# Gate and up projections of an FFN in seven half-size products instead of eight, in a tuned three-mixer layer kernel

## The reference

```python
x = x + g1 * _rmsnorm(mix, p['g_post_mix'])            # x1 below
h = _rmsnorm(x, p['g_pre_ffn']) * (1.0 + sc2) + sh2
f = (jax.nn.silu(h @ p['w_ffn_gate']) * (h @ p['w_ffn_up'])) @ p['w_ffn_down']
x = x + g2 * _rmsnorm(f, p['g_post_ffn'])
```

## Time and profile before

| | before |
|---|---|
| runs shown | 1843.31, 1847.68, 1849.92 us |
| median | 1847.68 us |
| the profiled execution's own time | 1849.39 us |
| its span | 1847.5 us (1.9 us lie around it) |
| mean granted TensorE clock | 0.98 of full speed |
| matmuls on PE | 12300 |

### The profile page before, as it was taken

One profiled execution on the slowest core, in us unless ns is written; L12 is line 12 of the kernel. 1 busy time (PEld: TensorE's weight loads), 2 busy tenths in 40 slices (PEclk: granted clock), 3 DMA queues, 4 the chain that ended last, 5 costly groups with the idle time before them and its releaser, 6 DMA issues.

```text
span 1847.5 us, 30614 instructions
## 1 busy us (share of the span) xinstructions
PE 1758.9 (95%) x12300; PEld 1645.6 (89%) x12300; DVE 879.7 (48%) x1584; ACT 587.1 (32%) x1209; POOL 108.4 (6%) x170
## 2 busy tenths in 40 slices
PE   5899899999999999999999899999899999999996
PEld 2678898898999999999997799999899999999995
DVE  2654425555465655333443344555564344434445
ACT  4333323333433332233333343232342222222222
POOL 0000101110122220000000000000000000000001
PEclk8899899999999999999999999999999999999998
DMA  9463232257623435754355745445223322322211
GB/s 344 152 245 124 79 116 94 79 174 216 217 89 130 140 128 177 249 164 141 119 163 185 251 168 179 157 147 168 92 69 103 92 69 69 87 74 69 90 49 57
DMA packets 237308, 254.65 MB, mean 138 GB/s; under 512 B 14983, under 2 KB 220487, under 8 KB 234096
## 3 DMA queue, kind: packets, MB, share of 16 engines
q1 hardware_dynamic: 208944, 223.85, 37.9%
q10 hardware_dynamic: 28224, 28.85, 4.6%
HBM read 194.11 MB, written 58.55 MB: 137 GB/s over the span
## 4 chain that ended last, share of the span: by engine, by line
PE 77%; issue 9%; DVE 5%; DMA 4%; DVEq 2%; ACT 1%; SPq 1%; POOLq 1%; POOL 0%; ACTq 0%; PEldq 0%; PEld 0%
PE pj_acc L374 14%; PE pj_acc L376 14%; PE pj_acc L375 14%; PE pj_acc L381 5%; PE pj_acc L382 5%; PE pj_acc L383 5%; PE mx L2796 3%; PE mx L2798 3%; PE mx L2797 3%; DMA ar_w<-in_w_ada 2%; PE mx L1753 2%; PE mx L2235 1%; PE mx L2244 1%; PE mx L1250 1%; PE mx L1263 1%
## 5 line engine op out<-in xcount | busy, mean ns | idle before, releaser
L374 PE MATMUL pj_acc<-pj_act_hi,pj_lo 128*128 128x320 f32 x1808 | 580.4, 321 | 5.1 <-DVE pj_act_lo L685 4.1
L375 PE MATMUL pj_acc<-pj_act_lo,pj_hi 128*128 128x320 f32 x1808 | 562.4, 311 | 0.0
L376 PE MATMUL pj_acc<-pj_act_hi,pj_hi 128*128 128x320 f32 x1808 | 562.3, 311 | 0.0
L374 PEld LDWEIGHTS pj_acc<-pj_act_hi,pj_lo 128*128 128x128 f32 x1808 | 343.4, 190 | 30.9 <-issue 26.6
L375 PEld LDWEIGHTS pj_acc<-pj_act_lo,pj_hi 128*128 128x128 f32 x1808 | 343.7, 190 | 4.3 <-issue 3.4
L376 PEld LDWEIGHTS pj_acc<-pj_act_hi,pj_hi 128*128 128x128 f32 x1808 | 343.0, 190 | 0.0
L342 DVE TENSOR_TENSOR pj_lo<-pj_raw,pj_hi 128x1024 fp32r<-128x1024 f32 (+1 forms) x196 | 241.5, 1236 | 160.2 <-ACT pj_hi L335 157.3
L335 ACT ACTIVATE pj_hi<-pj_raw 128x1024 fp32r<-128x1024 f32 (+1 forms) x196 | 205.1, 1053 | 231.6 <-PE mx L2798 116.2
L381 PE MATMUL pj_acc<-pj_lo,pj_act_hi 128*128 128x256 f32 x880 | 257.4, 293 | 6.1 <-DVE pj_tm_out L477 3.9
L382 PE MATMUL pj_acc<-pj_hi,pj_act_lo 128*128 128x256 f32 x880 | 251.1, 285 | 0.0
L383 PE MATMUL pj_acc<-pj_hi,pj_act_hi 128*128 128x256 f32 x880 | 251.0, 285 | 0.0
(11 more groups left out here) (370 smaller groups left out, 2140.0 us busy)
## 6 DMA issues: line engine op xcount, KB each, us to landing
pj_raw<-in_w_in SPq DMA_DIRECT2D x50, 1024.0 KB, 5.4
ar_w<-in_w_ada SPq DMA_DIRECT2D x16, 1024.0 KB, 5.6
pm<-pj_tm_out ACTq DMA_DIRECT2D x100, 128.0 KB, 2.5
pj_raw<-in_w_ffn_gate SPq DMA_DIRECT2D x22, 512.0 KB, 4.0
pj_raw<-in_w_ffn_up SPq DMA_DIRECT2D x22, 512.0 KB, 5.3
...
```

What stands on the lines that cost most here:

```text
L374: nc.tensor.matmul(out, lo[:, k, col], ahi[:, k, tok], start=(k == 0), stop=False)
L375: nc.tensor.matmul(out, hi[:, k, col], alo[:, k, tok], start=False, stop=False)
L376: last = nc.tensor.matmul(out, hi[:, k, col], ahi[:, k, tok], start=False, stop=(k == KT - 1))
```

## The change

**Seven products.** Up chunks 2 to 21 become "wino" chunks. The 1024 x 256 weight block is cut in four quarters of 512 rows x 128 columns, X(i, l) with i for gate or up and l for the k half, and the activations in four quarters of 4 k-tiles x 320 tokens. With sums of weight quarters and sums of activation quarters, the four results need 7 products of quarters instead of 8. A chunk then has 7 units (x = 0 to 6) of 4 x 3 = 12 matmuls of 128x320.

- The four sums of activation quarters are made once (steps "turned" 0 to 3, placed after units 3 to 6 of up chunks 0 and 1): DVE subtracts (L3074), ACT rounds (L3065), DVE makes lo (L3076), each 128x1280. For that Norm writes its result into a full-size buffer yf instead of tmp.
- The four sums of weight quarters are made in each chunk by DVE (Ffn.sum, L2916 to L2924, 128x512 each), three of them in place in raw. There are 7 blocks to split per chunk instead of 2 halves of 4 blocks.
- The results are put together after the products: ACT copies unit 1's bank to SBUF (P1), DVE makes seven 128x320 additions (L2973) into the buffers temps, ACT takes silu in place, DVE makes the two products (L2998), and hi and lo of f follow.

**Ring of blocks.** The two slots of hi and lo serve as a ring of eight blocks of 128x512. A wino chunk takes seven, a down chunk four; a block is split again as soon as its user is done.

**PSUM.** A wino chunk's units use banks 0, 1, 4, 2, 3, 0, 3 (WINO_BANK). The first 3 of the 10 down sums stay in banks 5 to 7 over all 11 down chunks and are copied out in the last; the other 7 use banks 0 to 3 in turn.

**Memory.** x1 no longer stays in SBUF: Norm makes it in the mix buffer, stores it to memory (L2725), and five loads (L2866) bring it back in the last down chunk. Norm's eviction of tile t waits for the store of tile t-2. The gate rows and their load move to the second to last down chunk. The last two down chunks run after wino chunk 21, next to each other.

The core of the diff:

```diff
+WINO_BANK = (0, 1, 4, 2, 3, 0, 3)
@@ Projection.tabulate
-            b = u % 2 if how != "down" else 2 + dn % 6
+            b = WINO_BANK[x] if how == "wino" else u % 2 if how != "down" else 5 + x if x < 3 else (x - 3) % 4
-            used[b] += 1
+            used[b] += how != "down" or x >= Ffn.HELD
...
+            if c.how in ("wino", "down"):
...
+                jobs = [(at + q,) for q in range(7)] if c.how == "wino" else [(at, at + 1), (at + 2, at + 3)]
...
+                for q, own in enumerate(jobs):
+                    own = [b % 8 for b in own]
+                    free = max(held[b] for b in own) + 1
+                    turn = max(turn, free)
+                    self.splits[turn].append((n, q))
+                    self.blocks[n, q], self.free_at[n, q] = own, free
+                    for c_half, b in enumerate(own):
+                        held[b] = self.first[n] + (q if c.how == "wino" else 8 + c_half)
@@ Projection.multiply
+        if c.how == "wino":
+            pe.wait_ge(self.lo_done, self.index[n, x] + 1)
@@ Ffn
+    def sum(self, dve, n, q):
+        X = lambda i, l: proj.quarter(n, i, l)
+        if q == 0:
+            dve.wait_ge(proj.loaded[proj.slot[n]], proj.load_count[n])
+            nc.vector.tensor_tensor(proj.block_source(n, 2), X(1, 0), X(1, 1), ALU.add).then_inc(E("sums"), 1)
+            dve.drain()
+            nc.vector.tensor_tensor(X(1, 0), X(0, 0), X(1, 0), ALU.subtract).then_inc(E("sums"), 1)
+        elif q == 3:
+            dve.drain()
+            nc.vector.tensor_tensor(X(0, 0), X(1, 1), X(1, 0), ALU.subtract).then_inc(E("sums"), 1)
+        elif q == 4:
+            dve.drain()
+            nc.vector.tensor_tensor(X(0, 1), X(0, 1), X(0, 0), ALU.subtract).then_inc(E("sums"), 1)
+    def multiply_quarter(self, pe, n, x, out, acc_full):
...
+            part = {2: 0, 4: 2, 6: 1, 3: 3}[x]
+            pe.wait_ge(self.m.sem("t_lo"), part + 1)
...
+        for k in range(4):
+            nc.tensor.matmul(out, wlo[:, k], ahi[:, k], start=(k == 0), stop=False)
+            nc.tensor.matmul(out, whi[:, k], alo[:, k], start=False, stop=False)
+            last = nc.tensor.matmul(out, whi[:, k], ahi[:, k], start=False, stop=(k == 3))
+    def dve_quarter(self, dve, u, n, x, acc, read):
...
+        elif x == 4:
+            dve.wait_ge(proj.acc_full, u + 1)
+            add(self.U, bank(4), self.P1).then_inc(free(4), 1)
+            dve.drain().then_inc(E("quarter"), 1)
+            add(self.W, bank(2), self.U)
+            dve.drain()
+        elif x == 5:
+            dve.wait_ge(proj.acc_full, u + 1)
+            add(self.G1, bank(5), self.W).then_inc(free(5), 1)
+            dve.drain().then_inc(E("quarter"), 1)
+        elif x == 6:
+            dve.wait_ge(proj.acc_full, u + 1)
+            add(self.V, bank(6), self.U).then_inc(free(6), 1)
+            dve.drain()
+            add(self.F0, bank(3), self.V).then_inc(free(3), 1)
+            add(self.F1, bank(2), self.V).then_inc(free(2), 1)
+            dve.drain()
@@ Norm.take
-            act.wait_ge(self.m.sem("x1"), t - 1)
+            act.wait_ge(self.m.sem("h"), t - 1)
+            act.wait_ge(self.m.sem("x1_out%d" % (t % 2)), 16 * (t // 2))
@@ layer, the plan
-        plan += [(ffn, s) for s in ffn.STEPS if (v == min(2 * s[1] + 3, 9) if s[0] == "last" else u == u_up + 20)]
+        at = {"turned": u_up + 3, "start": proj.first[ffn.spare] + 1, "rows": proj.first[ffn.spare] + 6,
+              "x1": proj.first[ffn.spare + 1]}
```

More of the change, by code:

```diff
@@ L298, in tabulate @@
         assert order == sorted(order), order
+        self.index = {job: k for k, job in enumerate([(0, 0), (0, 1)] + [job for sp in self.splits for job in sp])}
+        self.last_job = [max(q for j, q in self.index if j == n) for n in range(N)]
+        for u in range(U):
+            for n, q in self.splits[u]:
+                assert u < self.first[n] + (q if self.chunks[n].how == "wino" else 0) or u == 0, (u, n, q, self.first[n])
     def buffers(self, n):
@@ L324, in split_hi @@
     def split_hi(self, act, n, q):
+        if self.chunks[n].how in ("wino", "down"):
+            return self.block_hi(act, n, q)
         raw, hi, _ = self.buffers(n)
@@ L406, in act_unit @@
             self.act_store(act, u - 2)
+            if self.units[u - 2][1] == 6 and self.how(u - 2) == "wino":
+                self.ffn.split_hi(act, 2 * self.chunks[self.units[u - 2][0]].dst + 1, self.units[u - 2][0], 2)
         acc, read = self.out(u), self.read[self.bank[u]]
@@ L449, in act_late @@
             self.ffn.split_hi(act, self.nth[u] // 2, *self.units[u])
+        elif how == "wino" and self.units[u][1] == 6:
+            n = self.units[u][0]
+            self.ffn.split_hi(act, 2 * self.chunks[n].dst, n, 0)
     def act_store(self, act, u):
@@ L504, in dve_late, with dve_last @@
             self.ffn.split_lo(dve, self.nth[u] // 2, *self.units[u])
+    def dve_last(self, dve, u):
+        n, x = self.units[u]
+        if self.how(u) == "wino" and x == 6:
+            for half in range(2):
+                self.ffn.split_lo(dve, 2 * self.chunks[n].dst + half, n, 2 * half)
     def landed(self, eng, kinds, last):
@@ L2729 @@
     NG = FF // P
-    STEPS = [("start", 0)] + [("last", t) for t in range(NT)]
+    STEPS = [("turned", k) for k in range(4)] + [("start", 0), ("rows", 0), ("x1", 0)] + [("last", t) for t in range(NT)]
+    FIRST = 2
+    P1, U, V, W, G0, G1, F0, F1 = range(8)
+    HELD = 3
     def __init__(self, nc, m, norm, mod, g_post, y_rows, proj):
@@ new lines, in act_quarter @@
+    def act_quarter(self, act, u, n, x, acc, read):
+        E, nc, w = self.m.sem, self.nc, self.proj.chunks[n].dst - self.FIRST
+        if x == 1:
+            if w:
+                act.wait_ge(E("quarter"), 3 * (w - 1) + 2)
+            else:
+                act.wait_ge(E("t_lo"), 4)
+            act.wait_ge(self.proj.acc_full, u + 1)
+            nc.scalar.activation(self.temps[:, self.P1], acc, ACT.Copy)
+            act.drain().then_inc(read, 1)
+        elif x in (3, 6):
+            half = x // 4
+            act.wait_ge(E("quarter"), 3 * w + (3 if half else 1))
+            g = self.temps[:, self.G0 + half]
+            nc.scalar.activation(g, g, ACT.Silu)
+            act.drain().then_inc(E("silu"), 1)
@@ new lines, in dve_quarter @@
+    def dve_quarter(self, dve, u, n, x, acc, read):
+        E, nc, proj, w = self.m.sem, self.nc, self.proj, self.proj.chunks[n].dst - self.FIRST
+        bank, free = lambda q: proj.unit_out(n, q), lambda q: proj.read[WINO_BANK[q]]
+        add = lambda out, a, b: nc.vector.tensor_tensor(self.temps[:, out], a, self.temps[:, b], ALU.add)
+        if x == 1:
+            dve.wait_ge(free(1), proj.rank[u] + 1)
+            add(self.G0, bank(0), self.P1).then_inc(free(0), 1)
+            dve.drain().then_inc(E("quarter"), 1)
[8 more added lines that the diff above has]
+            add(self.G1, bank(5), self.W).then_inc(free(5), 1)
+            dve.drain().then_inc(E("quarter"), 1)
+        elif x == 6:
[5 more added lines that the diff above has]
+            dve.drain()
+            for half in range(2):
+                dve.wait_ge(E("silu"), 2 * (w + self.FIRST) + half + 1)
+                f = self.temps[:, self.F0 + half]
+                nc.vector.tensor_tensor(f, f, self.temps[:, self.G0 + half], ALU.mult)
+                dve.drain().then_inc(E("product"), 1)
@@ L2829, in dve_start, with t_part, act_turned, dve_turned @@
         dve.drain()
+    T_PARTS = ((0, 0), (0, 1), (1, 1), (1, 0))
+    def t_part(self, k):
+        l, half = self.T_PARTS[k]
+        return self.norm.yf[:, 4 * l:4 * l + 4, half * HALF:(half + 1) * HALF]
+    def act_turned(self, act, k):
+        E = self.m.sem
+        act.wait_ge(self.proj.acc_full, self.proj.first[self.proj.first_of("up")])
+        act.wait_ge(E("t"), k + 1)
+        self.nc.scalar.activation(self.t_hi[:, k], self.t_part(k), ACT.Copy).then_inc(E("t_hi"), 1)
+    def dve_turned(self, dve, k):
+        E, part = self.m.sem, self.t_part
+        a, b = ((1, 0), (2, 1), (2, 0), (3, 2))[k]
+        if k == 0:
+            dve.wait_ge(self.norm.m.sem("hi"), 2 * NT)
+        dve.drain()
+        self.nc.vector.tensor_tensor(part(k), part(a), part(b), ALU.subtract).then_inc(E("t"), 1)
+        dve.wait_ge(E("t_hi"), k + 1)
+        self.nc.vector.tensor_tensor(self.t_lo[:, k], part(k), self.t_hi[:, k].bitcast(F32), ALU.subtract
+                                     ).then_inc(E("t_lo"), 1)
     def act(self, act, step):
-        if step[0] == "start":
+        if step[0] == "turned":
+            return self.act_turned(act, step[1])
+        if step[0] != "last":
             return
@@ L2858, in dve @@
         E, nc, y = self.m.sem, self.nc, self.total[:, t]
[L2859 removed]
+        if step[0] == "turned":
+            return self.dve_turned(dve, t)
+        if step[0] == "rows":
             return self.dve_start(dve)
+        if step[0] != "last":
+            return
         dve.wait_ge(E("root"), t + 1)
```

(1 more changed line is left out.)

241 lines of the change are left out of this document (172 added, 69 removed).

## The result

The changed kernel takes **1823.55 us** (median of four runs, 1817.12 to 1828.40) against 1846.61 us before (1843.31 to 1849.92). The ratio is 0.987 with a 95% interval of 0.984 to 0.990. Forecast were 1822.7 us and a range of 1813 to 1835. Medians differ by 23.1 us; the pair of profiles differs by more, and most of that can be located.

What follows compares the result with a forecast made beforehand. PE was taken to bound the FFN by its number of matmuls. -36.95 + 8.7 + 1.7 + 1.0 + 0.5 = -25.0 us takes the median from 1847.7 to 1822.7 us, range 1813 to 1835.

Steps and rivals of the forecast that it cites:

- chunk 20: The wino chunk with all seven of chunk 21's splits where others have a down chunk's; charged 0.5 us.
- What is removed: 12 of 96 matmuls in each of 20 chunks, 35.2 us, and a 1.75 us wait before the last down chunk.
- DVE's load: DVE busy 32.7 us in a period of 38.6, 85% where it was 42%; on average it still fits.
- The margin of 0.2 us: In chunks before a down chunk, addition U is done at 10.2 us, 0.2 before PE needs bank 3 for unit 6.
- The count from end to end: Drain rule read strictly: U done at 10.5 us instead of 10.2, nine chunks losing about 1 to 2 us more.
- The front: First wino chunk, chunk 2: serial activation steps delay units 0 and 1, +8.7 us, bounds 5 and 11.
- The clock: PE's two waits at chunk 2 drop the clock to its lower level: +1.7 us, 0 to 3.4.
- The tail: The last down chunk takes 28.9 us to the end as before; if x1's first load were late, 2.5 us more.
- Changes at nothing: x1 stores and loads, weight loads and four banks for the last down sums were each expected to cost nothing.
- no stall at the front: Rival, chance 0.14: chunk 2 starts nearly on time, gain 33 to 37 us, 1811 to 1815.
- DVE late in even chunks: Rival, chance 0.15: each of nine chunks before a down chunk loses 0.5 to 1.5 us, 1828 to 1840.
- Slower than before: Rival, chance 0.04: late U pauses PE about 3 us in nine chunks and the clock falls each time; about 1864.

Runs made afterwards that it cites:

- x1_dup: Changed kernel with unit 0's 12 matmuls issued twice in each of the 20 wino chunks: 1850.66 us, ratio 1.001 to the kernel before.
- x2_extra2: Changed kernel with two more additions, a drain each, ahead of addition U on DVE in every wino chunk (1.16 us): 1837.72 us.
- m1_move: Changed kernel with activation step 3 placed one unit later, behind the product of unit 7: 1814.6 us in one run, FFN part 418.80.
- m2_pipe: Changed kernel with DVE issuing each next activation subtraction before it waits for ACT's rounding: 1817.75 us in one run, FFN part 418.87.
- x4_held0: Changed kernel with no down sum kept in PSUM, all ten added on DVE: 1813.39 us in one run, FFN part 422.62 against 422.65.
- m3_both: Changed kernel with the edits of m1_move and m2_pipe together: 1811.56 us, ratio 0.979 to the kernel before.
- x3_extra6: Changed kernel with six more additions, a drain each, ahead of addition U on DVE in every wino chunk (3.5 us): 1903.08 us.

## Why the prediction was right, point by point

The FFN part against before, by the terms of the sum. "Measured" is from the traces above.

| term | predicted | measured |
|---|---|---|
| 240 matmuls | -35.2 | -35.2 (pace 0.1466 us; two chunks 24.62 where two had 28.16) |
| wait ahead of the last down chunk | -1.75 | gone; by the starts it had cost 1.9 |
| front, waits | +8.7 | +9.1 |
| front, clock | +1.7 | +2.3 |
| chunks ahead of a down chunk | +1.0 | 0 |
| chunk 20 | +0.5 | +0.6 |
| tail | 0 | +1.0 |
| pace of down chunks | not seen | -2.0 |
| sum | -25.0 | -26.1 (the windows: -26.2) |

The mechanism was right: matmuls bound this part, their number carries the gain, and two waits at the front take part of it back. That the sum came out within 1.2 us owes something to luck: the pace of the down chunks (-2.0) and the chunks that cost nothing (-1.0) were missed on one side, the tail, the clock and the front's waits (+2.0 together) on the other. The median, 23.1 us down against 25.0 forecast, also holds the unsteady part ahead of the FFN.

- **What is removed** held to a tenth, and x1_dup shows that it is the cause.
- **DVE's load**: 31.0 us per period where 32.7 were counted. Of the 0.17 us of a drain, 0.09 is a gap between two instructions and no busy time, which is 2.0 us for the 22 of a period.
- **The margin of 0.2 us** was right: U was done at 1487.08 + 0.49 = 1487.57, 10.2 us behind the chunk's start. What I had set against so thin a margin, 1 us, wasn't spent, as the timeline repeats to 0.05 us from period to period. x2_extra2 confirms it (0.2), and adds what the prediction hadn't worked out: odd chunks have only about 0.5 us at the same bank. The count from end to end, 10.5 us, isn't what the trace shows; with it unit 6 would have paused in each even chunk. The section of the Trainium skill that the prediction cites for it (VectorE: DVE Perf Modes, The DRAIN you can't avoid) itself adds that a next instruction that is not held starts earlier. The trace agrees with that: the sum L2916 starts at 1485.08, 0.09 us ahead of the end of the split in front of it (1483.94 + 1.23).
- **The front**: unit 0 3.5 us late (3.2 predicted), unit 1 5.6 us later than unit 0's length would have it (5.4). m1_move and m2_pipe take away the two causes that were named, the position of step 3 and DVE standing still for ACT.
- **The clock** was mis-sized: I charged one piece of 3.4 us at the lower level and it was 13.7 us. That it came out near (2.3 for 1.7) is partly luck. Unit 0's slow run, 1.6 us longer than at full clock, hid in the wait for unit 1, and only the 4.9 us from unit 1's start to the clock's rise cost time. In x4_held0 and x2_extra2, where unit 1 starts as long behind unit 0 (7.33 us), the lower level lasted 10.2 us and cost some 1.8.
- **The tail** is 1.0 us longer. x1 came in time, as argued. Counted from the start of the last down chunk (1785.41), the last pair of L3119 starts 0.2 us later than the last pair of L2864 did before, since a token tile on DVE takes 4.37 us (1793.51 to 1797.88) where it took 4.28. The other 0.7 us lie behind that pair: the end comes 7.2 us after its start, before it came 6.5 after. In x2_extra2 and x4_held0 it comes some 6.85 after. Why, the runs don't show.
- **"Changes at nothing"**: no wait for the x1 stores, x1 loads, gate rows or weights shows behind 1380 us, and x4_held0 puts the sums in PSUM at 0.8 us at most. The x1 stores lie ahead of 1380 us, in the output projection, and cost it nothing either: from its first transpose on PE to the first matmul of up chunk 0 it takes 43.7 us (1315.19 to 1358.85), before it took 44.1 (1320.86 to 1364.93).
- **The rivals**: no stall at the front isn't what happened, but m3_both shows what it is worth, 9.6 us. DVE late in even chunks would have needed 0.2 us more. Slower than before needs more than the 1.16 us of x2_extra2, and 3.5 us are enough (x3_extra6).
